# Lo weights moved by 64 bytes, and an order of hi and lo products for each down projection

## The chip, the cores and the metric

The kernel runs on one core of a Trainium2 chip. The metric is the device time of one execution in microseconds, median of several runs. The engines are PE (TensorE, with its weight loads shown apart as PEld), DVE (VectorE), ACT (ScalarE), POOL (GpSimd) and SP, which issues the DMAs.

## What is computed

A stream x of 256 tokens by 1024 features passes two blocks, then two more of a second kind. All of it is float32.

```python
# first block, for l in 0, 1
x = x + (even_mixer if l == 0 else odd_mixer)(rmsnorm(x, norm_mix[l]))
x = x + swiglu(rmsnorm(x, norm_ffn[l]), w_gate, w_up, w_down)     # width 2816
# second block, for l in 0, 1 (layer norms with a residual factor between the parts)
x = swiglu_2 (width 4096), hybrid_mixer, swiglu_2 (width 4096)

def swiglu(h, w_gate, w_up, w_down):
    return (jax.nn.silu(h @ w_gate) * (h @ w_up)) @ w_down
```

The even mixer is a gated unit and latent attention, the odd mixer a retention, the hybrid mixer a delta rule and two local attentions. By far the most work is in the dense products, and there in the six gated feed-forward stages, called f0, f1, s00, t0, s01 and t1.

## The kernel before

**Products from two parts.** Every float32 operand is split into a hi part that fp32r holds exactly and a lo part, the rest. A product of weights and activations is then three: hi by hi, lo by hi, hi by lo. Weights arrive by DMA in chunks of 128 partitions by 1024 floats in six buffers `raw`; ACT copies them into `whi` (L1266), DVE subtracts for `wlo` (L2026), five buffers each. Activations stand in `xx` (hi and lo of one k side by side, 256 floats each), in `H` in the same form for the hidden units, and in `RX` for raw inputs of a layer norm (258 columns). All matmuls of the dense parts are issued by the helper at L452.

**Two forms.** The triplet form (`mm3`) issues three products of 256 columns per k. The wide form (`mm2`) streams hi and lo of the activations as 512 columns past the hi weights, then 256 hi columns past the lo weights: two products per k. It reverses their order from one k to the next, so the sequence reads hi, lo, lo, hi, hi, lo. A chunk of 1024 floats holds eight k of 128 columns. Each product loads its own 128 by 128 weights. In the value projections and in the last down projection (t1, `down_tokens`) it is the other way round: tokens are the stationary side and the weights move, 512, 384 or 324 columns at a time.

**Feed-forward.** `ffn` runs gate and up chunk by chunk, ACT and DVE make the hidden tile of `H` from them, and then the down projection takes eight rows of output, each over all k (22 or 32), waiting for `hlo` of each k.

**Layout.** `lay_memory` places the buffers; `line(past)` pads until the next address is `past` bytes beyond a multiple of 512. Before, `raw`, `whi`, `wlo` and `x` stand at 0, `xx` and `H` at 64, `RX` at 128 with slices of 1032 bytes.

**Start.** SP loads x as rows, then constants, then the packed vectors `pk`, then the first weights. PE transposes x in 16 matmuls (L1231), DVE copies the results (L2039, `take_in`), ACT writes xh and DVE xl (L2086, called xl below). Then `even` runs five chunks `ew_c` in the triplet form.

**Statistics.** `rms_stats` sums squares over the features by a product with a matrix of 1/1024. It is an fp32 product, which the trace shows as two records. Before, the squares stand in two tiles, so there are two products; with `RT` there is a transposed form too (stages e and o). Each retention head does likewise with `m.ones`.

The order of every engine's program is written out by hand; SP issues a chunk once `wlo` of the chunk six before it is made.

Of the kernel before, what the change touches and what calls it, by code (L numbers as in the profile page):

```python
# [14 lines left out]
ALPHA = float(4.0 ** 0.25)  # L15
NEG = -1e30
# [224 lines left out]
def lay_memory(nc, ctx, plan):  # L241
# [31 lines left out]
    line(0)  # L273
    m.wlo = sb("wlo", [128, NHL, CW], F32R)
    line(0)
# [16 lines left out]
    m.RX = nc.alloc_sbuf_tensor_at("RX", [128, 8, 2, 258], F32R, offset=at + 65600, align_bytes=64)  # L292
# [12 lines left out]
    m.xtm = c.get(2, 1024)  # L305
    m.sqt = arena[:, 0:2048]
# [39 lines left out]
    c = Carve(arena, nar, at=16432)  # L346
# [7 lines left out]
    names = ["x", "cst", "pk", "lvm", "out"] + [f"raw{i}" for i in range(NRAW)]  # L354
# [12 lines left out]
    "trx",  # L367
# [66 lines left out]
def tensor_program(e, m):  # L434
# [121 lines left out]
    def rms_stats(st, RT=False, last=1, bank=7):  # L556

        acc = [m.t8[0], m.t8[last]]
        w.wait_ge(s["acc"], st)
        if last == 7:  # L560
            w.wait_ge(s["xsq"], st, 7)
        b = take(bank, ("root", st))
        mm(b[:, 0:256], m.onm, acc[0], start=True, stop=False)
        mm(b[:, 0:256], m.onm, acc[1], start=False, stop=True).then_inc(s["stat"].h, s["stat"].up(st))
        if RT:
            b = take(6, ("root", st, "T"))
            for tt in range(2):
                sl = slice(tt * 128, tt * 128 + 128)
                mm(b[:, tt:tt + 1], acc[0][:, sl], m.onm[:, 0:1], start=True, stop=False)
                t = mm(b[:, tt:tt + 1], acc[1][:, sl], m.onm[:, 0:1], start=False, stop=True)  # L570
            t.then_inc(s["stat"].h, s["stat"].up(st, "T"))
# [16 lines left out]
    def gemm_raw(st, spec, at):  # L588

        def begin(n):
            name, i, b = spec(n)
            keys.append((name, i))
            parts.append((*weights(name, i), b))

        def tile(n, k):
            wh, wl, b = parts[n]
            c = k * 128
            a = m.RX[:, k]  # L600
            return mm3(b[:, 0:258], wh[:, c:c + 128], wl[:, c:c + 128], a[:, 0, :], a[:, 1, :], k == 0, k == 7)
# [12 lines left out]
        for n in range(split):  # L614
            tile(n, 7).then_inc(s["gemm"].h, s["gemm"].up(*keys[n]))
        for n in range(split, 6):
            begin(n)
            for k in range(8):
                t = tile(n, k)
                if (n, k) == (split, 1) and at == split - 1:  # L620
                    layer_norm(st)
            t.then_inc(s["gemm"].h, s["gemm"].up(*keys[n]))

    def down_tokens(st, wd):

        def tile(c, tt, wh, wl):
            b = bt[tt]
            for kk in range(2):
                k, cols, sl = c % 16 * 2 + kk, slice(kk * 512, kk * 512 + 512), slice(tt * 128, tt * 128 + 128)
                w.wait_ge(s["hlo"], st, k)  # L630
                mm(b[:, :], m.H[:, k, 0, sl], wh[:, cols], start=False, stop=False)
                mm(b[:, :], m.H[:, k, 1, sl], wh[:, cols], start=False, stop=False)
                t = mm(b[:, :], m.H[:, k, 0, sl], wl[:, cols], start=False, stop=k == 31)
            return t
# [20 lines left out]
        for c in range(12, 16):  # L655
            tile(c, 1, *wv[c - 12]).then_inc(s["gemm"].h, s["gemm"].up(wd, 16 + c))

    def ffn(st, wg, wu, wd, nt, kind, then, ln, at=0):
# [23 lines left out]
        for n in range(8):  # L682
            b = take(b0 + n % 4, ("xadd", then, n))
            for k in range(nt):
                if k % 8 == 0:
                    wh, wl = weights(wd, n * down_chunks(nt) + k // 8)
                w.wait_ge(s["hlo"], st, k)
                c = k % 8 * 128
                t = mm2(b, wh[:, c:c + 128], wl[:, c:c + 128], m.H[:, k], k == 0)
                if k % 8 == 7 or k == nt - 1:  # L690
                    t.then_inc(s["gemm"].h, s["gemm"].up(wd, n * down_chunks(nt) + k // 8))
            if ln and n == 2:
                centre(then, 4)
# [47 lines left out]
    def even():  # L741
# [27 lines left out]
        value(0)  # L769
        w.wait_ge(s["edve"], "kpf")  # L770
# [13 lines left out]
        w.wait_ge(s["gmw"], "in")  # L784
        b = take(3, ("eact", "gwT"))
        for g in range(4):
            t = e.transpose(b[:, g * 128:g * 128 + 128], m.gw[:, g, :], m.ident)
        t.then_inc(s["eps"].h, s["eps"].up("gw"))
# [86 lines left out]
    def odd():  # L875
        for cg in range(4):
            bq = [take(2 * (cg % 2) + tt, ("ract", "v", cg, tt)) for tt in range(2)]
            gemm_tm("ow_v", cg * 4, bq, xh, xl, 8, 2, 512, st="o")
            if cg == 0:
                rms_stats("o", RT=True, last=7)  # L880
# [5 lines left out]
        def head(h):  # L886
# [23 lines left out]
            mm(b[:, 0:256], m.ones, m.osq[:, 0, :], start=True, stop=False)  # L910
            mm(b[:, 0:256], m.ones, m.osq[:, 1, :], start=False, stop=True).then_inc(s["rps"].h, s["rps"].up("sum", h))
# [313 lines left out]
    w.wait_ge(s["cst"], "in")  # L1225
    w.wait_ge(s["x"], "in")
# [17 lines left out]
def scalar_program(e, m):  # L1244
# [58 lines left out]
    def rms_parts(st, gname, xin):  # L1303
        for p in range(4):
            w.wait_ge(s["xadd"], *xin, p)
            for k in (2 * p, 2 * p + 1):
                upper_x(st, gname, k)
        if st == "e":
            produce(3)
# [97 lines left out]
    def ffn(st, wg, wu, wd, nt, kind, tile, bname=None, first=0):  # L1407

        def raw(j):
            return kind == "ln" and j < 3  # L1410

        def hidden(j):
            w.wait_ge(s["fmul"], st, j)
            e.activation(m.H[:, j, 0, :], m.t2[:, j % 4, :], ACT.Copy, scale=-0.5 if raw(j) else 1.0).then_inc(  # L1414
                s["hhi"].h, s["hhi"].up(st, j))
# [84 lines left out]
    def even():  # L1500
        w.wait_ge(s["pk"], "in")
        rms_parts("e", "nm0", ("in",))
# [22 lines left out]
        w.wait_ge(s["eps"], "gw")  # L1525
        e.activation(m.gwT, four(3), ACT.Copy).then_inc(s["eact"].h, s["eact"].up("gwT"))
# [445 lines left out]

    w.wait_ge(s["set"], "onm")
# [25 lines left out]
def vector_program(e, m):  # L1999
# [36 lines left out]
    def take_in(p):  # L2036

        w.wait_ge(s["trx"], "in", p)
        e.tensor_copy(x[:, 2 * p:2 * p + 2, :], two(p)).then_inc(s["xadd"].h, s["xadd"].up("in", p))  # L2039

# [47 lines left out]

    def rms_behind(st, gname, gemm):

        def sum_up(p):
# [3 lines left out]
            t = e.tensor_tensor(m.sqs[0], m.sqs[0], m.sqs[p], ALU.add)  # L2095
            t.then_inc(s["acc"].h, s["acc"].up(st, p - 1) if p < 3 else s["acc"].up(st))
# [11 lines left out]
        sum_up(3)  # L2108

    def rms_parts(st, gname, gemm):  # L2110
        for p in range(4):
            if gemm is not None:
                add_pair(st, p, 1.0, gemm)
            for k in (2 * p, 2 * p + 1):
                lower_x(st, gname, k)
            if st == "e" and p < 2:
                take_in(p + 2)
        if st == "e":
            produce(3)
# [8 lines left out]
        e.tensor_tensor(acc, acc, m.sqs[3], ALU.add).then_inc(s["acc"].h, s["acc"].up(st))  # L2128

    def rms_tile(st, gname, n, gemm):  # L2130
# [3 lines left out]
        if gname is None or n in (0, 7):  # L2134
            return
        w.wait_ge(s["xsq"], st, n)
        if n > 1:
            w.wait_ge(s["acc"], st, n - 1)
        e.tensor_tensor(m.t8[0], m.t8[0], m.t8[n], ALU.add).then_inc(
            s["acc"].h, s["acc"].up(st, n) if n < 6 else s["acc"].up(st))  # L2140
# [212 lines left out]
    def ffn(st, wg, wu, wd, nt, kind, half, tile):  # L2353

        rms = kind == "rms"

# [24 lines left out]
        def hidden_low(j):  # L2381
            if kind == "ln" and j < 3:
                w.wait_ge(s["hhi"], st, j)
                e.scalar_tensor_tensor(m.H[:, j, 1, :], m.t2[:, j % 4, :], -half, m.H[:, j, 0, :].bitcast(F32), ALU.mult,
                                       ALU.subtract).then_inc(s["hlo"].h, s["hlo"].up(st, j))
                return
            low(m.H[:, j, 1, :], m.t2[:, j % 4, :], m.H[:, j, 0, :], ("hhi", "hlo"), st, j)
# [122 lines left out]
    def even():  # L2510
        w.wait_ge(s["pk"], "in")
        rms_parts("e", "nm0", None)
# [37 lines left out]
        w.wait_ge(s["eact"], "gwT")  # L2550
# [163 lines left out]
    def odd():  # L2714
# [36 lines left out]
        def head(h):  # L2751
            b = ps[5]
            w.wait_ge(s["rps"], "A", h)
            if h >= 2:
# [8 lines left out]
            e.tensor_tensor(m.osq[:, 0:2, :], m.osq[:, 0:2, :], m.osq[:, 2:4, :], ALU.add).then_inc(  # L2763
                s["rdve"].h, s["rdve"].up("sq", h))
# [390 lines left out]
    for p in range(2):  # L3155
        take_in(p)
# [88 lines left out]
def sync_program(e, m, ins, out):  # L3245
# [10 lines left out]
    def constants(c):  # L3256

        if c == 4:
            load("rowa", "in", m.rowc[:, 0:704], ins["rowa"].partition_broadcast(128))
            load("gmw", "in", m.gw, ins["gmw"].rearrange("g t s -> t g s"))  # L3260
# [37 lines left out]
def emit(nc, ins, out, plan):  # L3298

    with ExitStack() as ctx:  # L3300
# [8 lines left out]
        def _(e):  # L3309
            scalar_program(e, m)  # L3310
# [34 lines left out]
def lay_out(a):  # L3345

    d = {}
# [61 lines left out]
    d["gmw"] = a["gm_w_s"][0]  # L3409
# [3 lines left out]
    d["x"] = a["x"][0]  # L3413
# [60 lines left out]
```

## Time and profile before

| | us |
|---|---|
| median of 3 runs | 2294.93 (2294.81 to 2295.2) |
| the profiled execution | 2295.12 |
| its span in the profile | 2293.3 |
| PE busy in it | 2275.4 (99%) |
| PEld busy | 2060.9 (90%) |
| DVE busy | 1783.0 (78%) |
| ACT busy | 1287.0 (56%) |

Times below are from the profiled execution, counted from its start. A duration of PE ends with a modelled tail that overlaps the next matmul, so what one matmul costs is the distance between two starts. Rows of the timeline merge neighbours of one kind: x2 is two of them.

### The profile page before, as it was taken

What the parts mean: (1) busy time and instruction counts of PE and PEld (TensorE: products, weight loads), DVE (VectorE), ACT (ScalarE), POOL (GpSimd) and SP (SyncE); (2) the same over time, 40 slices, a digit from 0 to 9 for tenths busy, and PEclk for the clock granted to TensorE, in tenths of its full rate; (3) what the DMA queues carried; (4) which work ended last, traced back from release to release, by engine and by line L of the source; (5) the groups of instructions that cost most, each with busy time, mean ns of one, the idle gap of its engine ahead of it and who ended that gap; (6) DMA issues with size and microseconds to landing.
All of it is one profiled execution on the core that took longest, in us unless ns stands there. A gap on an engine that the chain in (4) does not pass through costs nothing.

```text
span 2293.3 us, 37657 instructions
## 1 busy us (share of the span) xinstructions
PE 2275.4 (99%) x15127; PEld 2060.9 (90%) x15127; DVE 1783.0 (78%) x2709; ACT 1287.0 (56%) x2017; POOL 79.7 (3%) x96
## 2 busy tenths in 40 slices
PE   8999999999999999999999999999999999999998
PEld 7988889998888888999999888998889999998887
DVE  6989658779859876797679886698767976798854
ACT  6855455655445554585656554455545856565542
POOL 0012000002100000020000000000000200000000
PEclk9999999999999999999999999999999999999999
DMA  6456565456556556654355555556665543556563
GB/s 229 141 186 196 190 203 172 153 162 208 183 177 211 193 188 190 201 180 137 120 184 183 195 191 182 178 193 204 186 195 195 182 139 121 177 182 218 188 184 99
DMA packets 115452, 412.45 MB, mean 180 GB/s; under 512 B 12880, under 2 KB 14800, under 8 KB 115024
## 3 DMA queue, kind: packets, MB, share of 16 engines
q1 hardware_dynamic: 114992, 407.96, 54.8%
q8 instruction: 120, 1.97, 0.4%
q0 software_dynamic: 288, 2.10, 0.3%
q14 instruction: 52, 0.43, 0.1%
HBM read 408.96 MB, written 1.05 MB: 179 GB/s over the span
## 4 chain that ended last, share of the span: by engine, by line
PE 88%; DVE 8%; ACT 2%; issue 1%; DMA 0%; SPq 0%; POOL 0%; DVEq 0%; ACTq 0%
PE ps L452 87%; DVE wlo L2026 3%; DVE region L2817 1%; ACT whi L1266 1%; ACT region L1487 1%; PE ps L725 0%; DMA raw<-in_ew_c 0%; DVE region L2348 0%; DVE RX L2218 0%; DVE x L2078 0%; DVE region L2351 0%; DVE x L2225 0%; DVE region L2463 0%; DVE region L2490 0%; DVE region L2986 0%
## 5 line engine op out<-in xcount | busy, mean ns | idle before, releaser
L452 PE MATMUL ps<-xx,whi 128*128 128x512 f32 (+1 forms) x4504 | 1204.3, 353 | 2.6 <-DVE wlo L2026 1.7
L2026 DVE TENSOR_TENSOR wlo<-raw,whi 128x1024 fp32r<-128x1024 f32 (+3 forms) x772 | 925.9, 1208 | 268.8 <-ACT whi L1266 266.8
L1266 ACT ACTIVATE whi<-raw 128x1024 fp32r<-128x1024 f32 (+3 forms) x772 | 801.0, 1043 | 520.9 <-PE ps L452 507.6
L452 PEld LDWEIGHTS ps<-xx,wlo 128*128 128x128 f32 x3696 | 694.3, 188 | 118.8 <-DVE wlo L2026 0.2
L452 PE MATMUL ps<-xx,wlo 128*128 128x256 f32 x3696 | 797.2, 279 | 0.0
L452 PEld LDWEIGHTS ps<-xx,whi 128*128 128x128 f32 x4504 | 691.5, 188 | 8.3 <-issue 4.9
L452 PE MATMUL ps<-H,whi 128*128 128x512 f32 (+1 forms) x2144 | 538.6, 339 | 0.1
L452 PE MATMUL ps<-H,wlo 128*128 128x256 f32 x1632 | 363.9, 279 | 0.0
L452 PEld LDWEIGHTS ps<-H,wlo 128*128 128x128 f32 x1632 | 306.5, 188 | 46.8
L452 PEld LDWEIGHTS ps<-H,whi 128*128 128x128 f32 x2144 | 329.4, 188 | 1.6 <-issue 0.8
L2021 DVE TENSOR_REDUCE t<-ps 128x256 f32<-128x512 f32 x320 | 219.8, 688 | 40.7 <-PE ps L452 36.5
L1414 ACT ACTIVATE H<-t 128x256 fp32r<-128x256 f32 x172 | 72.0, 418 | 96.3 <-DVE t L2379 41.7
L1449 ACT ACTIVATE t<-t 128x256 f32<-128x256 f32 x160 | 65.6, 410 | 60.2 <-DVE t L2419 33.0
L452 PE MATMUL ps<-whi,H 128*128 128x512 f32 (+1 forms) x296 | 91.8, 391 | 0.0
L452 PE MATMUL ps<-region 128*128 128x128 f32 (+9 forms) x944 | 89.4, 272 | 0.0
L452 PE MATMUL ps<-RX,whi 128*128 128x258 f32 x480 | 89.3, 285 | 0.0
L2049 DVE TENSOR_TENSOR H<-t,H 128x256 fp32r<-128x256 f32 x179 | 74.4, 419 | 10.5 <-ACT H L1414 7.3
L452 PEld LDWEIGHTS ps<-region 128*128 128x128 f32 (+5 forms) x944 | 76.0, 158 | 6.6
L452 PE MATMUL ps<-whi,xx 128*128 128x512 f32 (+1 forms) x288 | 79.4, 360 | 0.0
L452 PEld LDWEIGHTS ps<-RX,whi 128*128 128x128 f32 x480 | 75.5, 191 | 0.1
L3193 POOL TENSOR_TENSOR t<-t,R 128x256 f32<-128x256 f32 x44 | 53.6, 1219 | 561.2 <-ACT t L1449 561.2
L452 PE MATMUL ps<-RX,wlo 128*128 128x258 f32 x240 | 68.0, 283 | 0.0
(311 smaller groups left out, 1561.4 us busy)
## 6 DMA issues: line engine op xcount, KB each, us to landing
raw<-in_sg SPq DMA_DIRECT2D x128, 512.0 KB, 3.5
raw<-in_su SPq DMA_DIRECT2D x128, 512.0 KB, 3.5
raw<-in_sd SPq DMA_DIRECT2D x128, 512.0 KB, 4.0
raw<-in_mw_g SPq DMA_DIRECT2D x48, 512.0 KB, 3.5
raw<-in_fg SPq DMA_DIRECT2D x44, 512.0 KB, 3.2
raw<-in_fu SPq DMA_DIRECT2D x44, 512.0 KB, 3.3
raw<-in_fd SPq DMA_DIRECT2D x32, 512.0 KB, 3.5
raw<-in_mw_a SPq DMA_DIRECT2D x24, 512.0 KB, 4.1
```

Source lines behind the costliest of these rows:

```text
L452: return e.matmul(out, lhsT, rhs, start=start, stop=stop, skip_group_check=True)
L1266: e.activation(m.whi[:, c % NHL, 0:cw], m.raw[:, c % NRAW, 0:cw], ACT.Copy).then_inc(s["whi"].h, s["whi"].up(c))
L1414: e.activation(m.H[:, j, 0, :], m.t2[:, j % 4, :], ACT.Copy, scale=-0.5 if raw(j) else 1.0).then_inc(s["hhi"].h, s["hhi"].up(st, j))
L1449: e.activation(g, g, ACT.Silu).then_inc(s["silu"].h, s["silu"].up(st, j))
L1487: e.activation(S[:, i, sl], S[:, i, sl], ACT.Exp, bias=st[:, 1, c:c + 1], accum_out=st[:, 2, c:c + 1]).then_inc(s["aact"].h, s["aact"].up( ...
L2021: return e.tensor_reduce(dst, b[:, :].rearrange("p (a b) -> p b a", a=2), AX, ALU.add)
L2026: e.tensor_tensor(m.wlo[:, c % NHL, 0:cw], m.raw[:, c % NRAW, 0:cw], m.whi[:, c % NHL, 0:cw].bitcast(F32), ALU.subtract).then_inc(s["wlo"] ...
L2049: e.tensor_tensor(dst, src, hi.bitcast(F32), ALU.subtract).then_inc(s[sig[1]].h, s[sig[1]].up(*key))
L2817: e.scalar_tensor_tensor(y[:, d:256], pr[:, 0:256 - d], pk(f"cw{l}", 12 * (3 - d) + i), y[:, d:256], ALU.mult, ALU.add).then_inc(s["cdve"] ...
L3193: e.tensor_tensor(g, g, m.R[:, 0, :], ALU.mult).then_inc(s["fnrm"].h, s["fnrm"].up(st, j))
```

## The change

It has six parts. (1) `wlo` moves by 64 bytes, to the same place within 512 bytes as `xx` and `H`; `whi` stays. `RX` gets slices of 1152 bytes and moves by 64, and the last down projection uses `Hs`, which is `H` 64 bytes on. (2) The wide down projections are written by `row`, which takes `run` values of k at once, first all of one part and then all of the other, and turns the order around each time; `RUN` gives a number to each stage. (3) x arrives already as features by tokens, in two DMAs from ACT's queue, and the 16 transposes and four copies are gone; `pk` and the constants are loaded later. (4) Fourteen matmuls on a constant (`WARM`) stand at the start of PE's program. (5) DVE adds the last two tiles of squares (`two_to_one`, `rms_tile`, `head`), so that each statistic is one product. (6) The gating weights `gmw` arrive transposed, so four transposes and an ACT copy are gone.

```diff
+WARM = 14
+RUN = {"f0": 2, "f1": 1, "s00": 4, "t0": 8, "s01": 2}
...
     line(0)
     m.whi = sb("whi", [128, NHL, CW], F32R)
-    line(0)
+    line(64)
     m.wlo = sb("wlo", [128, NHL, CW], F32R)
-    line(0)
+    line(64)
     m.x = sb("x", [128, 8, 256])
     line(64)
     m.xx = sb("xx", [128, 8, 2, 256], F32R)
...
-    m.RX = nc.alloc_sbuf_tensor_at("RX", [128, 8, 2, 258], F32R, offset=at + 65600, align_bytes=64)
+    m.RX = nc.alloc_sbuf_tensor_at("RX", [128, 8, 2, 288], F32R, offset=at + 65664, align_bytes=64)
+    m.Hs = nc.alloc_sbuf_tensor_at("Hs", [128, 32, 2, 256], F32R, offset=at + 64, align_bytes=64)
...
-        mm(b[:, 0:256], m.onm, acc[0], start=True, stop=False)
-        mm(b[:, 0:256], m.onm, acc[1], start=False, stop=True).then_inc(s["stat"].h, s["stat"].up(st))
+        mm(b[:, 0:256], m.onm, acc).then_inc(s["stat"].h, s["stat"].up(st))
...
+    def row(st, b, wh, wl, c, ks, run):
+
+        for i in range(0, len(ks), run):
+            turn[0] ^= 1
+            for lo in (0, 1) if turn[0] or run == 1 else (1, 0):
+                for k in ks[i:i + run]:
+                    w.wait_ge(s["hlo"], st, 8 * c + k)
+                    o, wt = (b[:, 0:256], wl) if lo else (b[:, :], wh)
+                    a = m.H[:, 8 * c + k, 0, :] if lo else m.H[:, 8 * c + k].rearrange("p a b -> p (a b)")
+                    t = mm(o, wt[:, k * 128:k * 128 + 128], a, start=c == 0 and k == 0 and lo == (0 if turn[0] or run == 1 else 1),
+                           stop=False)
+        return t
...
-            mm(b[:, 0:256], m.ones, m.osq[:, 0, :], start=True, stop=False)
-            mm(b[:, 0:256], m.ones, m.osq[:, 1, :], start=False, stop=True).then_inc(s["rps"].h, s["rps"].up("sum", h))
+            mm(b[:, 0:256], m.ones, m.osq[:, 0, :]).then_inc(s["rps"].h, s["rps"].up("sum", h))
...
-    for p in range(4):
-        b = take(p, ("xadd", "in", p))
-        for kk in range(2):
-            for tt in range(2):
-                t = e.transpose(b[:, kk * 256 + tt * 128:kk * 256 + tt * 128 + 128],
-                                m.xtm[:, tt, (2 * p + kk) * 128:(2 * p + kk + 1) * 128], m.ident)
-        t.then_inc(s["trx"].h, s["trx"].up("in", p))
+    for _ in range(WARM):
+        mm(ps[7][:, 0:128], m.onm, m.onm)
...
+    for p in range(2):
+        e.dma_start(m.x[:, 4 * p:4 * p + 4, :], ins["x"][:, 4 * p:4 * p + 4, :]).then_inc(
+            s[f"x{p}"].h, s[f"x{p}"].up("in", by=16))
...
+    def two_to_one(st):
+
+        w.wait_ge(s["acc"], st, 2)
+        e.tensor_tensor(m.t8[0], m.t8[0], m.t8[1], ALU.add).then_inc(s["acc"].h, s["acc"].up(st))
...
+        if c == 1:
+            load("pk", "in", m.pk[:, :], ins["pack"])
+        if c == 3:
+            load("cst", "in", m.cst[:, :], c_[:, 0:768])
         if c == 4:
...
-    load("x", "in", m.xtm, ins["x"].rearrange("(a p) d -> p a d", p=128))
-    load("cst", "in", m.cst[:, :], c_[:, 0:768])
-    load("pk", "in", m.pk[:, :], ins["pack"])
```

DVE's program at the start. Before, the copies of x stand around the first split of weights and between the splits of x (`t` holds the squares):

```order
L2039 COPY x<-ps 128x512 x2
L2026 TENSOR_TENSOR wlo<-raw,whi 128x1024
L2086 SCALAR_TENSOR_TENSOR xx<-x,pk,xx 128x256 x2
L2039 COPY x<-ps 128x512
L2086 SCALAR_TENSOR_TENSOR xx<-x,pk,xx 128x256 x2
L2039 COPY x<-ps 128x512
L2086 SCALAR_TENSOR_TENSOR xx<-x,pk,xx 128x256 x4
L2026 TENSOR_TENSOR wlo<-raw,whi 128x1024 x3
```

Of the change, the same place:

```order
L2022 TENSOR_TENSOR wlo<-raw,whi 128x1024
L2077 SCALAR_TENSOR_TENSOR xx<-x,pk,xx 128x256 x8
L2022 TENSOR_TENSOR wlo<-raw,whi 128x1024 x3
L2114 TENSOR_TENSOR t<-t 128x512
L2117 TENSOR_TENSOR t<-t 128x512
L2120 TENSOR_TENSOR t<-t 128x512
L2083 TENSOR_TENSOR t<-t 128x256
```

The four copies are gone, and one addition of a single tile stands behind the three sums of squares.

PE's program where the down projection of t0 begins, after the last product of gate and up. Before:

```order
L452 MATMUL ps<-xx,whi 128x512
L452 MATMUL ps<-H,whi 128x512
L452 MATMUL ps<-H,wlo 128x256 x2
L452 MATMUL ps<-H,whi 128x512 x2
L452 MATMUL ps<-H,wlo 128x256 x2
```

Of the change:

```order
L453 MATMUL ps<-xx,whi 128x512
L453 MATMUL ps<-H,whi 128x512 x8
L453 MATMUL ps<-H,wlo 128x256 x16
L453 MATMUL ps<-H,whi 128x512 x16
L453 MATMUL ps<-H,wlo 128x256 x16
```

Eight k of one part follow each other, and with the turn sixteen; before it was one and two. In s00 they are four and eight, in f0 and s01 two and four, and in f1 hi and lo alternate one by one. The number of products is the same in all of them.

## Rows read from the trace of the kernel before

**Rows 1.** The page: busy time of each engine, share of the span and instructions.

```profile
PE 2275.4 (99%) x15127; PEld 2060.9 (90%) x15127; DVE 1783.0 (78%) x2709; ACT 1287.0 (56%) x2017; POOL 79.7 (3%) x96
```

**Rows 2.** PE's waits: us in total, times, longest; the view's first row.

```profile
PE ps L1231 <- DMA cst<-in_consts: 6.9, 1, 6.9
```

**Rows 3.** Timeline 0 to 18 us: start, duration, engine, operation, what ended its wait.

```profile
0.73 0.43 SPq L3251 DMA_DIRECT2D region<-in_x  x1
...
6.93 3.65 PE L1231 MATMUL ps<-cst,region 128*128 128x128 f32 x16 [6.93 <-DMA cst<-in_consts]
...
8.57 1.06 ACT L1266 ACTIVATE whi<-raw 128x1024 fp32r<-128x1024 f32 x1 [6.36 <-DMA raw<-in_ew_c]
...
9.66 1.23 DVE L2026 TENSOR_TENSOR wlo<-raw,whi 128x1024 fp32r<-128x1024 f32 x1
...
10.81 0.88 DVE L2086 SCALAR_TENSOR_TENSOR xx<-x,pk,xx 128x256 fp32r<-128x256 f32 x2
...
11.39 0.55 PE L452 MATMUL ps<-xx,whi 128*128 128x256 f32 x1 [0.81 <-DVE xx L2086]
...
16.96 0.36 PE L452 MATMUL ps<-xx,whi 128*128 128x256 f32 x1 [0.53 <-DVE wlo L2026]
```

**Rows 4.** DMAs before 12 us; windows: length, PE busy, clock, DMA share, GB/s.

```profile
region<-in_x SPq DMA_DIRECT2D x1, 1024.0 KB, 5.1
...
2.00:4.00 2.00, 0.00 (x0) 1.00 0.72 289
4.00:6.00 2.00, 0.00 (x0) 1.00 1.03 417
```

**Rows 5.** A wide stretch: its window, and timeline rows of PE at its beginning.

```profile
700.00:840.00 140.00, 140.00 (x813) 1.00 0.60 198
...
700.67 0.39 PE L452 MATMUL ps<-xx,wlo 128*128 128x256 f32 x2
700.89 0.62 PE L452 MATMUL ps<-xx,whi 128*128 128x512 f32 x2
701.35 0.40 PE L452 MATMUL ps<-xx,wlo 128*128 128x256 f32 x2
701.59 0.62 PE L452 MATMUL ps<-xx,whi 128*128 128x512 f32 x2
```

**Rows 6.** Timeline of PE, triplets of 256 columns: the first and the thirteenth.

```profile
426.46 0.28 PE L452 MATMUL ps<-xx,wlo 128*128 128x256 f32 x1
...
430.70 0.28 PE L452 MATMUL ps<-xx,wlo 128*128 128x256 f32 x1
```

**Rows 7.** Timeline of PE, raw form: the first and the ninth triplet.

```profile
945.77 0.40 PE L452 MATMUL ps<-RX,whi 128*128 128x258 f32 x2
...
948.66 0.41 PE L452 MATMUL ps<-RX,whi 128*128 128x258 f32 x2
```

**Rows 8.** Timeline of PE, weights moving past H: two starts six matmuls apart.

```profile
45.83 0.63 PE L452 MATMUL ps<-whi,H 128*128 128x512 f32 x2
...
47.23 0.63 PE L452 MATMUL ps<-whi,H 128*128 128x512 f32 x2
```

**Rows 9.** Statistics: timeline of PE in stage o, of DVE in stage f0.

```profile
303.30 1.03 PE L452 MATMUL ps<-t,onc 128*128 128x256 f32 x4
...
304.16 0.95 PE L452 MATMUL ps<-onc,t 128*128 128x1 f32 x8
...
118.91 1.75 DVE L2144 RECIPROCAL R<-t 128x256 f32<-128x256 f32 x1 [2.99 <-ACT t L1323]
```

**Rows 10.** Timeline of PE, 324 columns: four starts, each six matmuls on.

```profile
978.91 0.46 PE L452 MATMUL ps<-whi,xx 128*128 128x324 f32 x2
...
979.80 0.46 PE L452 MATMUL ps<-whi,xx 128*128 128x324 f32 x2
...
980.68 0.46 PE L452 MATMUL ps<-whi,xx 128*128 128x324 f32 x2
...
981.57 0.46 PE L452 MATMUL ps<-whi,xx 128*128 128x324 f32 x2
```

More of the change, by code:

```diff
@@ L352, in sig @@
         return Sig(ctx.enter_context(nc.semaphore(f"s_{name}")), plan and plan[name])
-    names = ["x", "cst", "pk", "lvm", "out"] + [f"raw{i}" for i in range(NRAW)]
+    names = ["x0", "x1", "cst", "pk", "lvm", "out"] + [f"raw{i}" for i in range(NRAW)]
     names += ["rowa", "gmw", "cs", "mk", "cc", "ss", "dtr", "rowc", "relb", "negd", "blk", "rowe"]
@@ L568, in rms_stats @@
                 sl = slice(tt * 128, tt * 128 + 128)
-                mm(b[:, tt:tt + 1], acc[0][:, sl], m.onm[:, 0:1], start=True, stop=False)
-                t = mm(b[:, tt:tt + 1], acc[1][:, sl], m.onm[:, 0:1], start=False, stop=True)
+                t = mm(b[:, tt:tt + 1], acc[:, sl], m.onm[:, 0:1])
             t.then_inc(s["stat"].h, s["stat"].up(st, "T"))
@@ L630, in tile @@
                 w.wait_ge(s["hlo"], st, k)
-                mm(b[:, :], m.H[:, k, 0, sl], wh[:, cols], start=False, stop=False)
-                mm(b[:, :], m.H[:, k, 1, sl], wh[:, cols], start=False, stop=False)
-                t = mm(b[:, :], m.H[:, k, 0, sl], wl[:, cols], start=False, stop=k == 31)
+                mm(b[:, :], m.Hs[:, k, 0, sl], wh[:, cols], start=False, stop=False)
+                mm(b[:, :], m.Hs[:, k, 1, sl], wh[:, cols], start=False, stop=False)
+                t = mm(b[:, :], m.Hs[:, k, 0, sl], wl[:, cols], start=False, stop=k == 31)
             return t
@@ L683, in ffn @@
             b = take(b0 + n % 4, ("xadd", then, n))
[L684 to L691, printed above, removed]
+            for c in range(down_chunks(nt)):
+                wh, wl = weights(wd, n * down_chunks(nt) + c)
+                t = row(st, b, wh, wl, c, range(min(8, nt - 8 * c)), RUN[st])
+                t.then_inc(s["gemm"].h, s["gemm"].up(wd, n * down_chunks(nt) + c))
             if ln and n == 2:
@@ L783, in even @@
         t.then_inc(s["esum"].h, s["esum"].up("rr"))
[L784 to L788, printed above, removed]
         def ukv(half):
@@ L879, in odd @@
             if cg == 0:
-                rms_stats("o", RT=True, last=7)
+                rms_stats("o", RT=True)
         for i in range(8):
@@ L1413, in hidden @@
             w.wait_ge(s["fmul"], st, j)
-            e.activation(m.H[:, j, 0, :], m.t2[:, j % 4, :], ACT.Copy, scale=-0.5 if raw(j) else 1.0).then_inc(
+            e.activation(H[:, j, 0, :], m.t2[:, j % 4, :], ACT.Copy, scale=-0.5 if raw(j) else 1.0).then_inc(
                 s["hhi"].h, s["hhi"].up(st, j))
@@ L2108, in rms_behind, with rms_parts @@
         sum_up(3)
-    def rms_parts(st, gname, gemm):
+        two_to_one(st)
+    def rms_parts(st, gname):
         for p in range(4):
-            if gemm is not None:
-                add_pair(st, p, 1.0, gemm)
+            w.wait_ge(s[f"x{p // 2}"], "in")
             for k in (2 * p, 2 * p + 1):
                 lower_x(st, gname, k)
[L2116 to L2119, printed above, removed]
+        produce(3)
         acc = m.sqs[0]
@@ L2383, in hidden_low @@
                 w.wait_ge(s["hhi"], st, j)
-                e.scalar_tensor_tensor(m.H[:, j, 1, :], m.t2[:, j % 4, :], -half, m.H[:, j, 0, :].bitcast(F32), ALU.mult,
+                e.scalar_tensor_tensor(H[:, j, 1, :], m.t2[:, j % 4, :], -half, H[:, j, 0, :].bitcast(F32), ALU.mult,
                                        ALU.subtract).then_inc(s["hlo"].h, s["hlo"].up(st, j))
                 return
-            low(m.H[:, j, 1, :], m.t2[:, j % 4, :], m.H[:, j, 0, :], ("hhi", "hlo"), st, j)
+            low(H[:, j, 1, :], m.t2[:, j % 4, :], H[:, j, 0, :], ("hhi", "hlo"), st, j)
         if kind != "ln":
@@ L3408, in lay_out @@
     d["rowa"] = np.concatenate([a["mla_q_norm"][0], a["mla_k_norm"][0], a["gm_b_s"][0].reshape(-1)])
-    d["gmw"] = a["gm_w_s"][0]
+    d["gmw"] = a["gm_w_s"][0].transpose(2, 0, 1)
     v = tm(a["w_ff2_out_2"][1], 2, 512).reshape(8, 4, 128, 1024)
@@ L3412, in lay_out @@
     d["rowe"] = np.stack([a["ln3_g_2"][1], a["ln3_b_2"][1]])
-    d["x"] = a["x"][0]
+    d["x"] = a["x"][0].T.reshape(8, 128, 256).transpose(1, 0, 2)
     return d
```

58 lines of the change are left out of this document (25 added, 33 removed).

## The prediction

> **What bounds the kernel now.** I read the page first. PE is busy for 99% of the span and the weight loads for 90%; no other engine passes 78% [rows 1]. Then PE's own waits: the longest by far is 6.9 us before its first instruction [rows 2]; four more kinds follow it, all shorter and none of them for H. So almost nothing waits: the time is the number of matmuls multiplied by their spacing, plus a start. Only four things can move it: fewer matmuls, closer spacing, an earlier start, or a new wait.
>
> Durations of PE rows overlap, so a price is read from start to start. In the wide form (512 hi columns, 256 lo columns) 813 matmuls lie in 140 us, 172 ns each, where their columns at 2.4 GHz are 160 ns [rows 5]. Twelve triplets of 256-column products (hi by xh, lo by xh, hi by xl) take 4.24 us (426.46 to 430.70), 353 ns a triplet, or 118 ns each where the columns are 106.7 [rows 6]. Eight triplets of the raw form (RX, 258 columns) take 2.89 us, 361 ns a triplet [rows 7]. With the weights moving, six of 512 columns take 1.40 us, 233 ns each where the columns are 213 [rows 8]. Every product that changes its weights thus pays 10 to 20 ns above its columns. Addresses and order could touch that part, and the program has 13637 fp32r matmuls to pay it.
>
> **The start.** x arrives as rows, is transposed in 16 matmuls from 6.93 us on, copied by DVE and split into xh and xl; the first real product starts at 11.39 and the second chunk of weights at 16.96, when its wlo is there [rows 3]. The change drops transposes and copies, and issues x in two halves from ACT's queue, beside SP's first chunk. DMA moves 289 GB/s from 2 to 4 us and 417 after that [rows 4]. Before, x landed 5.1 us after its issue at 0.73 [rows 3, 4], so at 5.8, when 1.34 MB had moved. Afterwards half of x and the first chunk are 1.05 MB at the head of both queues: moved by 5.1, landed by some 5.9. Then whi of chunk 0 (1.06) to 7.0, wlo (1.23) to 8.25, the first xl (0.42) to 8.7: the first product at 8.75. pk is 0.18 MB behind chunk 0 and lands near 6.8, before ACT needs it. DVE paces the first chunk with eight xl at 0.42, to 11.6; its next wlo is done at 12.85, so the second chunk starts at 12.9 and not at 16.96: **-4.0 us**. From there PE is fed as before, in the same order. (whi, wlo and xl by the durations of [rows 3].) The clock matters here: sixteen transposes of 128 columns take 3.65 us, over 0.2 each [rows 3], twice what 2.4 GHz would need, although the granted clock of that stretch reads 1.00; the triplets at 426 us run at 2.4 GHz [rows 6]. The 14 warm-up matmuls are fp32 products of two passes, at most 28 x 0.21 = 6 us from 1.2 on, so they end by 7.2 and delay nothing. If the clock is still low at 8.75, a k costs 0.64 us and not 0.42, chunk 0 ends at 13.9 and the gain is 3.0. I take 4.0, as they are ordinary products and run until just before.
>
> The page TensorE: Matmul & The Clock Gate of the Trainium skill (Part 4: PE-mode transpose) says that transposes do not count as work for the clock. The trace agrees as far as it goes: 3.65 us is fifteen spacings of 0.21 and the last one's own 0.42, so none of the sixteen ran faster [rows 3]. By that rule the old start had no warm-up at all, which speaks for the 4.0.
>
> **Matmuls removed.** A statistic of two fp32 products becomes one. One such product is two records of 0.215 us (four start within 0.86) [rows 9], so 0.43 each: stages e, o, f0 and f1, **-1.7 us**. The transposed statistic of e and o drops four records of some 0.10 us each time (eight take 0.95 with the last one's tail) [rows 9]: **-0.8**. The four retention heads drop one fp32 product of 256 columns each: **-1.7**. The four transposes of the gating weights, at half the spacing of those at the start: **-0.45**. DVE gets eight additions of one tile in their place, by xl's row 0.42 us each. Their cover is DVE's idle time: before the reciprocal of f0's statistic it had idled 2.99 us [rows 9], and no wait of PE names these sums. Without cover each would cost 0.5 us, 4 in all. In stage e the statistic comes right after the third chunk, both sides shift by about 4 us, and I allow nothing for it.
>
> **The layout.** xx and H start 64 bytes past a multiple of 512, whi and wlo on one. Every slice of weights is 512 bytes and every slice of xx 2048, so each weight load stood at one distance (64) from the stream beside it. Now wlo is at distance 0 and whi stays at 64: 5568 lo loads change, by the program's count. The trace has no such load at distance 0. Nearest are the 324-column products, whose moving weights start 0, 272 and 32 bytes past a line in turn: six of them take 0.89, 0.88 and 0.89 us [rows 10]. So distance is worth at most 0.01 us in six, 1.7 ns each: between -9.3 and +9.3 us for 5568. Wider ends come from the wide form: a pair of lo products takes 0.22 or 0.24 us in alternation [rows 5]. The program has 4000 k in the wide form, so 2000 such pairs, and 1560 triplets. All pairs at 0.22 is 5 ns off the mean, or -10 us; with as much on each triplet -18. All pairs at 0.24, and the triplets at RX's price less its columns (+5 ns), is +18. The surcharge is 11 ns at the old distance, 13 at RX's shifting ones; there is more room below than seen above, so I take half a nanosecond: **-2.8**. That value is chosen; the row only bounds it.
>
> RX moves to whole lines (1152 bytes a slice, no longer 1032). Its triplet costs 361 [rows 7] where 354 [rows 6] plus 2.5 for six more columns would be 356.5: 240 triplets at 4.5 ns are 1.1 us if alignment is the reason and 0 if not: **-0.6**. Hs shifts H by 64 in the last down projection alone, 384 products of 233 ns that lie inside the bound above.
>
> The page SBUF — State Buffer of the Trainium skill (Who interferes with whom) gives PE two independent read ports, one for the stream and one for weight loads, and says PE never waits on anyone. By it no address matters, both layout terms are 0, and the sum would be -8.65: 2286.3. No run here shows distance 0, so this stays a rival.
>
> **The order of hi and lo.** Only down projections change: f1 alternates, f0 and s01 go by pairs, s00 by fours, t0 by eights. Products and loads keep their number. From the wide rows, hi after hi and lo after lo cost no more than the switches (a hi pair 0.46, a lo pair 0.22 to 0.24) [rows 5], which gives 0. The other bound is 233 for a 512-column product in a row of its own size [rows 8] and 118 for 256 [rows 6]: 351 a k against 345, on the 944 k of f0, s00, t0 and s01, **+5.7**. I take 0, since the switches are the same kind of instruction in the same rows. A run of eight asks for hlo of the last k 0.9 us sooner; no wait of PE names H's lo part, so there is slack of unknown size.
>
> **The sum.** -4.0 -1.7 -0.8 -1.7 -0.45 -2.8 -0.6 = -12.05. The profiled execution took 2295.12 (2293.3 of span and 1.8 around it), 0.2 over the median of 2294.93. So the forecast is **2283**.
>
> **Rivals.** (a) Addresses count for nothing: 2286.3, as above; for it speak the 324-column rows. (b) The new distance is the fast one for most lo loads: -18 in place of -2.8, 2268. For it: the alternating 0.22 and 0.24, so a faster state exists. Against: nothing ties it to addresses. (c) Slower: distance 0 makes stream and lo load collide; the surcharge would have to rise by 2.5 ns on each of 5568 loads (13.9 us) before the kernel is slower by over 0.2%; at the +18 bound it is 2304. For it: lo pairs at 0.24 exist. Against: 324-column rows allow 1.7. (d) Runs cost what the 512-column stream says: +5.7, 2288.6. (e) The early start is given back at a later wait, since weights must land 4 us earlier: 2287; against it, chunks wait in the queue for free buffers, not for bandwidth (DMA share 0.60 in the wide stretch [rows 5]).
>
> **How the numbers follow.** Forecast with small layout effects 0.40 (2279 to 2286), a 0.14, b 0.23, c 0.11 (half of it short of slower), d 0.07, e 0.05. The range runs from 2268 (b) to 2291, into c; it leaves out some 0.2. 0.2% is 4.6 us, about what a measurement of this kernel tells from no change: faster below 2290.3. Case c is 0.06 slower and 0.05 within; 0.03 more within, for sums that fall short: faster 0.86, within 0.08, slower 0.06.
>
> **What would show it.** The first real product near 8.8 and the second chunk near 12.9. Statistics with two records where there were four. The 700 to 840 stretch with 813 matmuls if spacing stands, 818 or more under b, 808 or fewer under c. Runs of eight in t0 at 345 a k or at 351. Wrong would be a hi-lo pair that moved by more than 3 ns, or PE waits for DVE's added sums.

## The result and the profile after

The changed kernel takes 2302.0 us (2301.85 to 2303.01), the kernel before 2294.93 in the same rounds. The ratio is 1.0031, with an interval of 1.002 to 1.0042: slower by 7 us, where 12 us less were forecast. It lies outside the stated range.

From the page of the changed kernel, the span and the busy times, to be held against [rows 1]:

```profile
span 2300.4 us, 37627 instructions
...
PE 2287.1 (99%) x15111; PEld 2065.4 (90%) x15111; DVE 1784.7 (78%) x2713; ACT 1286.2 (56%) x2016; POOL 79.9 (3%) x96
```

PE has 16 records fewer and is busy 12 us longer. The waits did not grow. This is PE's list of waits (us in total, times, longest), for [rows 2]:

```profile
PE ps L453 <- DVE xx L2077: 2.1, 1, 2.1
PE ps L453 <- DVE wlo L2022: 1.2, 4, 0.4
PE ps L453 <- DVE onc L3151: 1.2, 1, 1.2
PE ps L731 <- ACT region L1488: 1.1, 3, 0.4
PE ps L453 <- DVE R L2198: 0.8, 2, 0.4
PE ps L453 <- DVE t L2083: 0.3, 1, 0.3
```

They come to 6.7 us, less than the first row alone had before. So matmuls start further apart, and the question is which. Both traces hold the same dense products in the same number, so both can be cut at the same products and each length taken from start to start. Summed by kind, in us (negative is shorter than before). "Start" runs to the end of the five chunks `ew_c` and holds stage e's sums; "wide on xx" is gate and up together with the wide products of the two other mixers; the last column holds the other fp32 sums and transposes that went away:

| kernel | start | wide on xx | down f0 | f1 | s00 | t0 | s01 | RX | tokens stationary | triplets | all the rest |
|---|---|---|---|---|---|---|---|---|---|---|---|
| before, its lengths | 30.1 | 995.5 | 60.7 | 60.7 | 88.3 | 88.3 | 88.3 | 89.9 | 186.9 | 466.5 | 131.2 |
| changed | -4.0 | +13.5 | +0.3 | -0.8 | +1.0 | +1.0 | +0.5 | -0.3 | -0.7 | +0.6 | -4.0 |

The start, the dropped products and the token products all shrink. The wide products on xx, whose code the change does not touch, grow by 13.5 us, 12.2 of them in gate and up. Windows of two such stretches (length, PE busy, clock, DMA share, GB/s), for the window of [rows 5]:

```profile
140.00:220.00 80.00, 80.00 (x458) 1.00 0.61 201
700.00:840.00 140.00, 140.00 (x804) 1.00 0.60 195
```

The second held 813 matmuls before and holds 804. From start to start, a chunk of eight k (16 products) took 2760 ns in the kernel before: 336 of the 360 chunks on xx do so to within one ns. In the changed kernel none does: most take 2792 to 2795, about 2800 or 2826 to 2828. The timeline of PE in f1, where they take 2827:

```profile
519.82 0.39 PE L453 MATMUL ps<-xx,wlo 128*128 128x256 f32 x2
520.05 0.64 PE L453 MATMUL ps<-xx,whi 128*128 128x512 f32 x2
520.52 0.39 PE L453 MATMUL ps<-xx,wlo 128*128 128x256 f32 x2
...
521.23 0.39 PE L453 MATMUL ps<-xx,wlo 128*128 128x256 f32 x2
```

A pair of lo products and the pair of hi products behind it now take 0.71 us (519.82 to 520.52, and 520.52 to 521.23), against 0.68 and 0.70 in [rows 5]. In the same kernel the down projection of f1 is faster than in the kernel before. Timeline of PE there:

```profile
625.48 0.39 PE L453 MATMUL ps<-H,whi 128*128 128x512 f32 x1
625.70 0.28 PE L453 MATMUL ps<-H,wlo 128*128 128x256 f32 x1
625.82 0.39 PE L453 MATMUL ps<-H,whi 128*128 128x512 f32 x1
...
626.84 0.39 PE L453 MATMUL ps<-H,whi 128*128 128x512 f32 x1
```

Four k take 1.36 us (625.48 to 626.84), 340 ns each: a chunk is 2720. This is the only stage that alternates hi and lo one by one, and it is where the experiments began.

The start came out near the forecast. Timeline of the first 14 us, for [rows 3]:

```profile
1.18 5.59 PE L453 MATMUL ps<-onc 128*128 128x128 f32 x28 [1.18 <-DVE onc L3151]
...
6.15 1.06 ACT L1260 ACTIVATE whi<-raw 128x1024 fp32r<-128x1024 f32 x1 [3.01 <-DMA raw<-in_ew_c]
...
7.24 1.23 DVE L2022 TENSOR_TENSOR wlo<-raw,whi 128x1024 fp32r<-128x1024 f32 x1 [6.11 <-ACT whi L1260]
...
8.38 3.25 DVE L2077 SCALAR_TENSOR_TENSOR xx<-x,pk,xx 128x256 fp32r<-128x256 f32 x8
...
8.91 0.38 PE L453 MATMUL ps<-xx,whi 128*128 128x256 f32 x1 [2.15 <-DVE xx L2077]
...
13.25 0.40 PE L453 MATMUL ps<-xx,whi 128*128 128x256 f32 x2
```

The first product starts at 8.91 (8.75 was forecast) and the second chunk at 13.37 (12.9 forecast, 16.96 before); the row at 13.25 is the last product of the first chunk and the first of the second. At the second chunk the gain is 3.6; behind stage e's statistic, which is shorter too, it is 4.0 and stays there. The single statistics, in stage o:

```profile
300.45 0.59 PE L453 MATMUL ps<-t,onc 128*128 128x256 f32 x2
300.89 0.50 PE L453 MATMUL ps<-onc,t 128*128 128x1 f32 x4
301.25 0.71 PE L453 MATMUL ps<-whi,xx 128*128 128x512 f32 x2
```

Two 256-column records take 0.44 us (300.45 to 300.89) where four took 0.86 [rows 9], and four of one column stand where eight did.

### The profile page after: what moved, and what is told of

It is laid out like the page before. It is cut to its first block, busy times and chain, and to the rows that moved or that the text cites. A ratio compares the mean times of both kernels' runs of the same rounds, so it can differ in the third digit from the quotient of the medians.

```text
span 2300.4 us, 37627 instructions
## 1 busy us (share of the span) xinstructions
PE 2287.1 (99%) x15111; PEld 2065.4 (90%) x15111; DVE 1784.7 (78%) x2713; ACT 1286.2 (56%) x2016; POOL 79.9 (3%) x96
## 4 chain that ended last, share of the span: by engine, by line
PE 89%; DVE 8%; ACT 2%; issue 1%; DMA 0%; SPq 0%; POOL 0%; DVEq 0%; ACTq 0%
PE ps L453 88%; DVE wlo L2022 3%; DVE region L2814 1%; ACT whi L1260 1%; DMA raw<-in_ew_c 0%; PE ps L731 0%; ACT region L1482 0%; DVE region L2341 0%; DVE RX L2211 0%; DVE x L2069 0%; DVE region L2344 0%; DVE x L2218 0%; DVE region L2983 0%; DVE region L2450 0%; DVE region L2980 0%
## 5 line engine op out<-in xcount | busy, mean ns | idle before, releaser
L453 PE MATMUL ps<-H,whi 128*128 128x512 f32 (+1 forms) x2144 | 492.9, 339 | 0.1
L453 PEld LDWEIGHTS ps<-H,whi 128*128 128x128 f32 x2144 | 359.8, 188 | 33.9 <-issue 0.6
L453 PE MATMUL ps<-H,wlo 128*128 128x256 f32 x1632 | 330.4, 281 | 0.0
L453 PEld LDWEIGHTS ps<-H,wlo 128*128 128x128 f32 x1632 | 263.2, 189 | 13.7
L1409 ACT ACTIVATE H<-t 128x256 fp32r<-128x256 f32 x140 | 58.5, 418 | 75.2 <-DVE t L2373 29.5
L453 PE MATMUL ps<-whi,Hs 128*128 128x512 f32 x256 | 79.8, 392 | 0.0
L2040 DVE TENSOR_TENSOR H<-t,H 128x256 fp32r<-128x256 f32 x150 | 62.2, 419 | 9.0 <-ACT H L1409 5.8
```

The source lines that it names most:

```text
L453: return e.matmul(out, lhsT, rhs, start=start, stop=stop, skip_group_check=True)
L1409: e.activation(H[:, j, 0, :], m.t2[:, j % 4, :], ACT.Copy, scale=-0.5 if raw(j) else 1.0).then_inc(s["hhi"].h, s["hhi"].up(st, j))
L2040: e.tensor_tensor(dst, src, hi.bitcast(F32), ALU.subtract).then_inc(s[sig[1]].h, s[sig[1]].up(*key))
```

## The experiments

Lengths of stretches are measured from start to start as above. Each kernel is the changed one with the edit shown, if nothing else is said.

**Only wlo back.** `x`, which stands behind it, moves with it here and in the next run.

```diff
-    line(64)
+    line(0)
     m.wlo = sb("wlo", [128, NHL, CW], F32R)
-    line(64)
+    line(0)
     m.x = sb("x", [128, 8, 256])
```

> The changed kernel with wlo and x back on a multiple of 512; order of the down projections, start, sums, RX and Hs stay changed. Distance theory: the 13 us that the wide gate and up stretches gained in length come from the lo loads at distance 0, so they return (a chunk of eight k back from some 2810 to 2760 ns) and the kernel ends near 2288. Order theory: the loss is made by the down projections' new order and what it leaves behind, so the gate and up stretches stay long and the kernel ends near 2301.

2287.8 us, 0.9968 of the kernel before (0.9957 to 0.998) and 14.2 below the changed kernel. Its window at 700 us:

```profile
700.00:840.00 140.00, 140.00 (x814) 1.00 0.62 197
```

The count is about that of before, and 334 of the 360 chunks are at 2760 again. The distance theory's number, 2288, came out. The down projections, which keep their new order, are within 0.2 us of the old ones, except f1's alternation, which costs 0.7.

**Only the place, in the kernel before** (the same two lines as above, the other way, in the kernel before).

> The kernel before with wlo and x moved by 64 bytes and nothing else. Distance theory: the wide xx stretches grow by 12 to 14 us, the triplets stay, and the wide down projections grow too, by 1 to 1.5%, in all some 2311. Order theory: the time stays at 2295.

2313.75 us, 18.5 more. Wide products on xx +12.7, the five down projections +4.9 together, triplets +0.7, all else +0.2. The same window of it:

```profile
700.00:840.00 140.00, 140.00 (x802) 1.00 0.60 196
```

The loss of the changed kernel stands here alone and whole, and larger. In both runs `x` moved beside `wlo`, and no run moves `x` alone; the wide products read no `x`, and further down, with `x` kept at 64, a move of `whi` alone changes the time by 38 us (2310.72 against 2272.32).

**The old order, in the changed kernel.** All runs are 1 and the turn is made at each k.

```diff
-RUN = {"f0": 2, "f1": 1, "s00": 4, "t0": 8, "s01": 2}
+RUN = {"f0": 1, "f1": 1, "s00": 1, "t0": 1, "s01": 1}
...
-            for lo in (0, 1) if turn[0] or run == 1 else (1, 0):
+            for lo in (0, 1) if turn[0] else (1, 0):
...
```

> The changed kernel with every down projection back in the old order (hi lo, lo hi, turned at each k), layout as changed. If the runs of 2, 4 and 8 cost by themselves as the 233 ns stream said, the down projections get 3 us shorter: 2299. If they make up for part of what the layout costs, the down projections get longer, by some 1% of 88 us in each of s00, t0 and s01: 2303. Gate and up stretches unchanged by both.

2308.72 us, 6.7 more than the changed kernel. The down projections add 4.3 us (f0 +0.6, f1 +2.3, s00 +0.5, t0 +0.2, s01 +0.7). The other 2.1 come in gate and up, whose code is the same: the stretch behind f1's down projection takes 4.3 us more than before in this kernel and 2.1 in the changed one. So the same products at the same places can be spaced differently. What ran before them differs here, but this kernel was run once, and a run below shows such a difference without any edit ahead of it; that the order in f1 made these 2.1 us is not shown. Both expectations were off by a few us, and both took gate and up as unchanged; the sign is that of the second.

**whi moved too.** `whi` and `wlo` both 64 past a line.

> The changed kernel with whi also 64 bytes on, so that hi and lo loads both stand at distance 0 from xx and H. If distance 0 costs each load the same, hi loads now pay as well: another 10 us or more, triplets longer too, 2312 or above. If what costs is that hi and lo weights differ in their place within 128 bytes, the loss goes away: near 2288.

2306.58 us. Neither expectation held as a whole. A chunk on xx takes 2786 to 2787, so the wide products on xx take 4.1 us less than in the changed kernel; the five down projections, of the wide form too, take 3.9 more, and the triplets 5.4 more. A fixed price on each load at distance 0 would have lengthened the whole wide form, and its sum did not move; only the triplets got longer, as the first expectation said.

**The plain order, hi then lo, in every wide product.**

```diff
     def mm2(b, wh, wl, a, start):
 
-        turn[0] ^= 1
+        turn[0] = 1
...
-RUN = {"f0": 2, "f1": 1, "s00": 4, "t0": 8, "s01": 2}
+RUN = {"f0": 1, "f1": 1, "s00": 1, "t0": 1, "s01": 1}
```

> The changed kernel, layout as changed, but every wide product (gate, up and all down projections) in the plain order hi, lo, hi, lo, with no turn and no runs. In the changed kernel's f1, the one stage with that order, a chunk of eight k took 2720 ns, against 2760 of the kernel before and 2793 to 2827 of its gate and up stretches. Interplay theory (the lo place and the order decide together): all 500 wide chunks go to 2720, the kernel to some 2268 to 2275. Distance theory (distance 0 costs each lo load by itself, f1 is short for another reason): the gate and up stretches stay at 2793 or more and the time stays at 2300 or above.

2272.32 us, 0.9894 of the kernel before (0.9877 to 0.991): 30 us below the changed kernel with the same layout and the same products. Windows of f0 and at 700 us:

```profile
140.00:220.00 80.00, 80.00 (x459) 1.00 0.60 201
700.00:840.00 140.00, 140.00 (x826) 1.00 0.59 199
```

The second holds 826 matmuls, the first no more than in the changed kernel. PE's timeline there and at 700 us:

```profile
140.03 0.40 PE L453 MATMUL ps<-xx,whi 128*128 128x512 f32 x1
140.27 0.28 PE L453 MATMUL ps<-xx,wlo 128*128 128x256 f32 x1
140.38 0.40 PE L453 MATMUL ps<-xx,whi 128*128 128x512 f32 x1
...
141.44 0.40 PE L453 MATMUL ps<-xx,whi 128*128 128x512 f32 x1
```

```profile
700.23 0.39 PE L453 MATMUL ps<-xx,whi 128*128 128x512 f32 x1
700.45 0.28 PE L453 MATMUL ps<-xx,wlo 128*128 128x256 f32 x1
700.57 0.39 PE L453 MATMUL ps<-xx,whi 128*128 128x512 f32 x1
...
701.59 0.39 PE L453 MATMUL ps<-xx,whi 128*128 128x512 f32 x1
```

In f0 hi and lo take 232 and 118 ns (medians): four k are 1.41 us (140.03 to 141.44), a chunk 2800. At 700 us they take 227 and 113, four k 1.36 (700.23 to 701.59), a chunk 2720. f1, whose code is that of f0, has the short spacing. One of the four executions took 2267.15 where the three others took 2272.3. Of the 488 wide chunks of eight k in the traced one 408 were at 2720 and 60 at 2800.

**The plain order with wlo back.**

> The same plain order hi, lo, hi, lo everywhere, with wlo and x back on a multiple of 512. f1 of the run with only wlo put back took 2790 a chunk. Interplay theory: 500 chunks at 2790, some 12 to 15 us more than with the turned order, 2300 to 2303. If the plain order were good by itself: 2720 a chunk, near 2268.

2316.69 us: the slowest of all, 44 us above the run before it, by 64 bytes. Most chunks take 2822 to 2825 or 2831 to 2832, more than the 2790 expected. The timeline of PE at 700 us, each row the start of a k:

```profile
700.11 0.39 PE L453 MATMUL ps<-xx,whi 128*128 128x512 f32 x1
...
700.45 0.40 PE L453 MATMUL ps<-xx,whi 128*128 128x512 f32 x1
...
700.81 0.40 PE L453 MATMUL ps<-xx,whi 128*128 128x512 f32 x1
...
701.17 0.39 PE L453 MATMUL ps<-xx,whi 128*128 128x512 f32 x1
```

The k are 0.34, 0.36 and 0.36 us apart, where the run before it has 0.34 throughout.

**Both back.** Place and order as before; start, sums, gating weights, RX and Hs as changed.

> Both the place of wlo and the order of the down projections as before; what is left of the change is the start, the single sums, the transposed gating weights, RX and Hs. My sum for these was -9.3 us, 2286. The runs of 2, 4 and 8 at the old place cost or give at most 1 us by the run with only wlo put back, whose time was 2287.8; f1's plain order cost 0.65 there, so this one should come to 2287.

2286.93 us, 8.1 below the kernel before: start -4.0, RX -0.2, tokens -0.3, triplets +0.3 and all the rest, the dropped sums and transposes, -3.9. The wide chunks, on xx and on H, are as before, 338 of 360 on xx at 2760. The expectation was 2287. With three other runs this gives place and order against each other, all else being as changed (us):

| | turned order | plain order |
|---|---|---|
| wlo at 0 | 2286.93 | 2316.69 |
| wlo at 64 | 2308.72 | 2272.32 |

The place alone costs 21.8 us and the order alone 29.8; if the two were independent, both would give 2338.5, and they gave 66 us less. Three of the four are one execution each; the largest difference seen between executions of one kernel here is 5.2 us, far below 66.

**wlo at 128.** `wlo` is laid before `raw`, 128 past a line. `raw` and `whi` stand further on by a multiple of 512, and `x` is at 0 again, as in the kernel before.

> The changed kernel with wlo 128 bytes past a multiple of 512, so that it stands 64 from xx on the other side, an odd number of lines as before the change. If only the parity of the distance in lines of 64 bytes counts, the wide stretches return to 2760 a chunk and the time to 2288. If the distance itself counts, or the place of wlo against whi, they take some other value.

2304.68 us. Chunks on xx of 2813 to 2814 (294 of them) and 2773 to 2774 (42), none at 2760; the triplets are 2.8 us shorter than before and the token products 2.2. The parity of the distance alone does not decide.

**The plain order at three other places.** whi and wlo at 64:

> Plain order, whi and wlo both 64 past a multiple of 512 (distance 0 from xx for both loads). In the turned order this layout took 2786 a chunk, between the 2760 of the old layout and the 2793 of the changed one. If what makes the plain order short is that hi and lo weights stand in different lines of a pair, this one stays at 2786 or more: 2305. If it is that lo loads meet their stream at distance 0, it goes to 2720 as well, and the time to 2285 since its triplets cost 4 us more.

whi at 64, wlo at 0:

> Plain order, places of whi and wlo exchanged: whi 64 past, wlo on a multiple of 512; hi loads at distance 0, lo loads at 64. If only the difference between the two matters it is as short as the changed layout, 2720 a chunk and 2272. If the long stream needs the odd distance in front of it, it is as slow as or slower than the plain order at the old places (2789 to 2832 a chunk): 2316.

wlo at 128:

> Plain order with wlo 128 past a multiple of 512: 64 from xx on its other side, an odd number of lines, as whi. If parity of lines decides, it behaves as with wlo on the multiple: 2789 to 2832 a chunk, 2316. The turned order at this place took 2813 and 2773 where the old place took 2760, so parity alone already does not explain that one; 2750 or less here would drop it.

2310.72, 2307.21 and 2298.13 us. In the second of them the two buffers also change their order in memory. Put together, the length of a chunk on xx in ns, by place and order (the values that occur most):

| whi, wlo past a line | turned order | plain order |
|---|---|---|
| 0, 0 | 2760 | 2823 to 2832, some 2789 to 2793 |
| 0, 64 (the change) | 2793 to 2800, 2826 | **2720**, or 2800 |
| 64, 64 | 2786 | 2773, 2819, 2830 |
| 64, 0 | not run | 2800, 2804, 2809, 2813 |
| 0, 128 | 2813, 2773 | 2773, 2826 |

With both at 64 nothing reaches 2720, but 146 chunks fall to 2773, below the 2786 that the other branch of its expectation named. The exchange of places falls between its two. At 128 most chunks (218) are at 2773: less than the 2789 to 2832 that parity asked for, though not the 2750 that was named as dropping it.

**One product more.** The plain order and the changed layout, with one 256-column product, overwritten by the next, before the third gate chunk of f0.

```diff
-    def gemm_wide(name, i, b):
+    def gemm_wide(name, i, b, extra=False):
         wh, wl = weights(name, i)
+        if extra:
+            mm(b[:, 0:256], wl[:, 0:128], m.xx[:, 0, 0, :])
...
-                gemm_wide(wg, j, bank(j, 0))
+                gemm_wide(wg, j, bank(j, 0), st == "f0" and j == 2)
```

> The plain order with the changed layout and one more product (256 columns on lo weights, its result overwritten by the next one) before the third gate chunk of f0. In the run without it f0's wide part ran at 2800 a chunk (232 and 118 ns) and every later one at 2720 (227 and 113), and one execution of four was 5.2 us shorter. If the two spacings are two states that a stretch keeps until something disturbs it, the extra product may set f0 to 2720: 2267. If f0 is slow for a reason of its own (its banks, its buffers), nothing changes but 0.1 us: 2272.4.

2266.96 us (2266.89 to 2267.01), 0.9877 of the kernel before (0.986 to 0.9893). Window of f0:

```profile
140.00:220.00 80.00, 80.00 (x472) 1.00 0.64 208
```

f0 now holds 472 matmuls in 80 us where it held 459, and 338 chunks on xx are at 2720. The kernel is 5.4 us shorter, the fastest version of all. That looks like the expectation come true, but the trace takes the cause away from the added product. It stands at 116.0 us, and f0 had the short spacing from its first wide product on. PE's timeline there, four k apart, without the added product:

```profile
108.45 0.40 PE L453 MATMUL ps<-xx,whi 128*128 128x512 f32 x1
...
109.86 0.40 PE L453 MATMUL ps<-xx,whi 128*128 128x512 f32 x1
```

The same four k in the kernel with it, and the added product, which is one of the two lo products in the last row:

```profile
108.42 0.39 PE L453 MATMUL ps<-xx,whi 128*128 128x512 f32 x1
...
109.78 0.39 PE L453 MATMUL ps<-xx,whi 128*128 128x512 f32 x1
...
115.90 0.40 PE L453 MATMUL ps<-xx,wlo 128*128 128x256 f32 x2
```

1.41 us against 1.36, over 6 us before the added product, in code that is the same. So the two spacings are two states of one sequence, and which one f0 takes was settled before the added product ran. With 2267.15 in one of four executions of the kernel without it and 2267 in all four with it, chance is not ruled out, and what settles it stays open.

## Why the prediction was wrong, point by point

**The start (-4.0 forecast).** 3.6 us at the second chunk. The total of -4.0 holds stage e's shorter statistic as well, forecast at 0.8 apart, of which 0.35 came: PE waited 0.3 us for the added sum. So start and stage e gave 4.0 where 4.8 were forecast. DVE idled 0.32 us for ACT's second whi before the second wlo (its row at 11.96), which the sum had left out. The clock was another step that did not go as taken. Windows of PE (length, busy, granted clock):

```profile
5.00:5.50 0.50, 0.50 (x4) 1.00 0.97 259
6.00:6.50 0.50, 0.50 (x7) 1.00 1.04 414
8.90:12.40 3.50, 3.49 (x17) 0.55 1.02 414
12.50:16.00 3.50, 3.50 (x31) 0.98 1.05 395
```

The warm-up products start 0.21 us apart until 5.8 and 0.11 apart behind it (a window also counts records that began before it). They end at 6.8, and PE idles 2.15 us for xl. Then the granted clock is 0.55, and the triplets are 0.64 us apart, until 12.4. The first chunk ended at 13.3. What that cost is seen in the run with the old order, whose first chunk was at the fast spacing in all but a few products. Its second chunk, in PE's timeline:

```profile
13.27 0.39 PE L453 MATMUL ps<-xx,whi 128*128 128x256 f32 x1 [0.92 <-DVE wlo L2022]
```

It waits 0.92 us for wlo and starts at 13.27 against 13.37, so the low clock cost 0.1 us; DVE paces the start. The prediction's price for it, 1.0 us, let PE be the slower of the two. The kernel before had the same 0.64 us a triplet until about 15.1 without a warm-up, so these runs do not show that the warm-up gained anything; no run leaves it out.

**Matmuls removed (-1.7, -0.8, -1.7, -0.45).** Right outside stage e: 3.8 us of the 4.65 belong there, and with both place and order put back the sums and transposes come to -3.9. The one wait that came of it is 0.3 us for the sum of `two_to_one` in stage e (`t`, L2083 in the list above). The whole of these with the start is -8.1 measured, against -9.25 in the sum (with RX).

**RX (-0.6).** -0.2 to -0.3. Eight triplets on whole lines, for [rows 7]:

```profile
944.55 0.40 PE L453 MATMUL ps<-RX,whi 128*128 128x258 f32 x2
...
947.44 0.40 PE L453 MATMUL ps<-RX,whi 128*128 128x258 f32 x2
```

2.89 us, as before: alignment was not the reason for their price.

**The layout (-2.8): this step failed, and it alone turned the gain into a loss.** It measured +14.2 us, the changed kernel's 2302.0 against 2287.8 with wlo (and x) put back. It was priced as a cost of each lo load that depends on its distance from the stream, bounded by the 324-column rows to 1.7 ns and taken on the side of a gain, because "there is more room below than seen above". The runs showed instead that place and order act together. At the old order the move costs 33 to 67 ns for eight k, at the plain order it saves 103 to 112 on most chunks, and triplets hardly notice (+0.7 us in the run with the place alone). The 324-column rows gave no bound for wide products: they stream weights, and lie in another sequence. Rival (c) had the sign and the size of its threshold: 18.5 us over 5568 loads is 3.3 ns each, past its 2.5. But 17.6 us of it fell on the 4000 lo loads of the wide form, 4.4 each, and at the plain order the same place makes chunks shorter, so a fixed price for each load that meets its stream is not the mechanism. Rival (b), a faster state at the new distance, did not come in this kernel; the state exists (2720 a chunk) and needed the plain order.

**The order of hi and lo (0).** Wrong as a sum of its own. At the old place the runs are worth 0.2 us a stage, as taken, and the +5.7 of the 512-column stream did not appear. At the new place they save 4.3 us in the down projections; another 2.1 in the stage behind f1 go with them in the one run there is. The change gave its new order to the down projections and left the wide products on xx, 995 us, in the turned one, which is the wrong one at the new place.

**Rival (a)**, that no address matters, falls: moving `wlo` and `x` by 64 bytes, and nothing else, made the kernel 18.5 us longer. The prediction based it on the Trainium skill (SBUF — State Buffer, Who interferes with whom: two independent read ports, PE waits on no one). No trace here shows PE waiting for another engine in these stretches either; the place shows in the spacing instead. **Rivals (d) and (e)** did not occur: (d)'s price is missing at the old place (0.2 us a stage), and no later wait gave the early start back, apart from the 0.3 us in stage e.

**What stays open** is the mechanism. The runs show that the spacing depends on the places of whi and wlo, on the sequence of long and short streams, and on a state that can differ between stages and executions of the same code. They do not show what in the array or in the memory makes it so, nor what picks the state. Parity of 64-byte lines and a fixed price per distance, each taken alone, do not fit the runs. Most of these runs are one execution, so a difference of up to some 5 us between two of them proves little by itself.

## What to carry to other kernels

When PE is busy for 99% and nothing waits, measure start to start over one repeated unit of the loop: units that agree to a nanosecond show a state, and a few ns per matmul decide the result. Try buffer places and issue order together, since each alone was a loss here (21.8 and 29.8 us) and both together a gain of 15 to 20 beside the same kernel. Change every loop of the same form, not the one at hand, and look at each stage for the wider of two spacings before calling a version finished. Before crediting an edit with such a gain, look whether it was there already ahead of the edit.

## What the runs showed of the hardware

64 bytes in the place of one weight buffer (and of x behind it) moved the whole kernel by 44 us (2316.69 against 2272.32) at the same instructions. With whi at 0 and wlo at 64, alternating products of 512 and 256 columns ran at 227 and 113 ns or at 232 and 118, for a whole stage, in identical code: f0 had the second in one kernel's trace and the first in another's, before the place where the two kernels differ. After 5.6 us of products on a constant, whose spacing had fallen from 0.21 to 0.11 us, PE idled for 2.15 us, and the next 3.5 us were granted 0.55, close to the lower of the two levels (0.5, 1.2 GHz).
